# One 64-token chunk left out of the last levels of a blocked triangular inverse, in a two-block model on one Trainium2 core

## The chip, the cores and the metric

The kernel runs on one core of a Trainium2 chip, as a single program. A core has a matrix engine (TensorE, in the profile PE, its weight loads PEld), a vector engine (VectorE, DVE), a scalar engine (ScalarE, ACT), GpSimd (POOL), and SyncE (SP), which here only issues DMA transfers. Each engine works through its own instruction stream in order and waits on semaphores that the others raise. The metric is the device time of one execution in microseconds (us), as the median of several runs; lower is better.

## What is computed

Two model blocks run one behind the other on 512 tokens of width 1024. The first has an RWKV-7 mixer (32 heads of 64) and a latent attention mixer; the second a convolution and Fourier mixer and a grouped-query attention mixer. Only the RWKV-7 scan matters here. 16 learned tokens stand ahead of the 512 of the input, so it runs over 528 tokens:

```
h = jnp.concatenate([meta, x], axis=1)          # 16 + 512 tokens
...
def _wkv7_scan(r, decay, k, v, a_vec, b_vec):   # per head, S is 64 x 64
    def step(S, inp):
        r_t, w_t, k_t, v_t, a_t, b_t = inp
        sa = jnp.einsum('bhij,bhj->bhi', S, a_t)
        S = S * w_t[:, :, None, :] + sa[..., None] * b_t[:, :, None, :] + v_t[..., None] * k_t[:, :, None, :]
        return S, jnp.einsum('bhij,bhj->bhi', S, r_t)
```

Inside a chunk of 64 tokens this recurrence can be solved at once: with N the strictly lower triangular 64x64 matrix of products of a and b, the chunk needs the inverse of (I - N), and after that only the state S is handed from chunk to chunk.

## The kernel before

The program has a chain of stages. Stage A (a loop over 16 pairs of heads, L572) makes the projections of every pair and stores the forms of a pair (a, r, b, k, v, gate, bonus, per chunk) in HBM. **Stage B** (`pe_pass`, `act_pass`, `dve_pass`, `pool_pass`) is the recurrent stage. Stage C (from L1097 on) and those behind it are projections, attention and the second block, and this change doesn't touch them.

Stage B takes a pair of heads at a time: one head on partitions 0 to 63, the other on 64 to 127 (`by_head` issues each matrix product once for either head). 528 tokens are padded in front by PAD = 48 to LP = 576, which makes NC = 9 chunks of C = 64. So the first chunk has 48 empty tokens and 16 real ones. The chunks are handled in GROUPS = 3 groups g of GC = 3 chunks; `grp(g)` are a group's chunks and `flat(g)` its columns. `group(out, lhsT, rhs, chunks, done)` (L756 to L759) issues the products of all its chunks into one PSUM bank.

The stage is a sequence of passes, `passes(eng, body)`: pass i handles three pairs at once, the forms, inverse and a, k, b, v rows of pair i (`inv`), the walk over the nine chunks with the state of pair i - 1 (`scan`), and the normalisation of pair i - 2 (`post`). Passes 0 and 1 are written out, the passes 2 to 15 are the body of a loop of 7 turns with two passes each (L1037), passes 16 and 17 are written out again. `schedule` writes the order of the items of a pass by hand and `merged` spreads the 18 steps of the walk evenly among them; every engine goes through the same list and does what it has to do of each item.

The items that matter here, for pair i:
- `rows` n: product with the identity that turns a form into token rows; n = 0 to 2 are v, 3 to 5 k, 6 to 8 b, 9 to 11 a. ScalarE copies them out (L905), a into `a_tok` (in the profile a_rows).
- The inverse is built by doubling. `start` makes W (`xw[:, W_OF + par]`), GpSimd makes X and `n_lvl[:, lv]`, which are N masked to the blocks that join at level lv = 0 to 4 (blocks of 2, 4, 8, 16 and 32 tokens). Then at every level: `E` (lv, g) multiplies N of the level by W into `inv_bank[g]` and ScalarE copies it to `e_all` (L912); `XW` (lv, g) multiplies X by E (the corrections of X, into the bank's first half, not at the last level) and E by X (those of W, into the second half), and VectorE adds both halves to X and W in one instruction (L976), at the last level W alone (L979). In the profile X and W are the tile x_w and all PSUM banks are "wide".
- `A` g multiplies the a rows by W into a_hat (L915), which the walk of the next pass uses from chunk 1 on (L777: `if c > 0`).
- the walk of chunk c: products into u, y and state, ScalarE copies u (L889) and y (L892), VectorE updates the state (L943, L946, L949).

The matrices are 32-bit. In the profile a 64x64 product of one head stands as two weight loads (PEld) and two matmuls (PE), so that one product of a group of three chunks for both heads is a row of "x12". GpSimd (the masked N and X) and SyncE (the loads of forms) do in every pass what they did.

## Time and profile before

| | us |
|---|---|
| median of 3 runs | 2703.03 |
| lowest and highest of them | 2698.32 and 2703.87 |
| the profiled execution | 2701.88 |
| its span, first to last instruction | 2700.1 |

| stretch of the span | what runs | PE busy |
|---|---|---|
| 0 to 540 us | norm, stage A | 484.89 |
| 540 to 1345 us | stage B, the recurrent stage | 632.12 |
| 1345 to 2700 us | stage C and all behind it | 1160.08 |

The views used below are: a table of the engines' busy time in chosen stretches, with the granted TensorE clock; the chain of work that ended last, in order of time; the DMA queues of a stretch; the timeline, which merges equal instructions that follow each other (start, length in us, what, x count, and in brackets the engine's idle time ahead of it and what ended it); the waits, grouped; and groups of instructions with their mean duration. "issue" is time in which an engine waited for nothing that the profile shows. Instruction code that the engines fetch appears as a DMA queue of the kind "instruction".

### The profile page before, as it was taken

How to read it: one execution, taken by the hardware profiler on the slowest of the kernel's cores; microseconds unless marked ns; L12 is line 12 of the kernel's file. 1: busy time of each engine (PE TensorE's matmuls, PEld its weight loads, DVE VectorE, ACT ScalarE, POOL GpSimd, SP SyncE). 2: the span in 40 equal slices, each digit the busy share in tenths (PEclk: the TensorE clock that was granted, in tenths of full speed). 3: DMA queues.
4: the chain of work that ended last, by engine and by line, in shares of the span. 5: the costliest groups of instructions: out<-in, count | busy, mean ns of one | idle time of the engine just before them, and what ended most of it. 6: DMA issues, size and time to landing. Idle time of an engine off the chain costs nothing.

```text
span 2700.1 us, 67991 instructions
## 1 busy us (share of the span) xinstructions
PE 2277.1 (84%) x27094; PEld 1973.2 (73%) x27094; DVE 1338.5 (50%) x1907; ACT 786.2 (29%) x1899; POOL 1204.8 (45%) x708
## 2 busy tenths in 40 slices
PE   6799999987787887777686799999989499888776
PEld 5698898877777777777685796777779376565555
DVE  6666666634444444444444631445431544538655
ACT  1623323333333333333321222233311202111331
POOL 1465665531312213113385682222167588675234
PEclk8899999999999999999797899999989799999998
DMA  2234343431212112111221122000012221121001
GB/s 81 88 148 157 134 163 143 148 122 34 78 43 72 52 43 81 43 48 55 103 80 54 55 86 70 32 31 16 31 47 93 73 93 62 63 70 59 28 0 62
DMA packets 66824, 198.59 MB, mean 74 GB/s; under 512 B 26784, under 2 KB 29088, under 8 KB 62240
## 3 DMA queue, kind: packets, MB, share of 16 engines
q1 hardware_dynamic: 66592, 195.24, 20.8%
q8 instruction: 177, 2.90, 0.4%
q14 instruction: 55, 0.45, 0.1%
HBM read 156.24 MB, written 38.99 MB: 72 GB/s over the span
## 4 chain that ended last, share of the span: by engine, by line
PE 75%; DVE 10%; issue 8%; ACT 4%; POOL 1%; DVEq 0%; ACTq 0%; DMA 0%; SPq 0%; POOLq 0%
PE wide L754 22%; PE wide L1146 11%; PE wide L1147 11%; PE wide L1148 11%; PE wide L1622 4%; PE wide L355 4%; PE wide L1718 2%; PE wide L1682 2%; PE wide L1683 1%; PE wide L1507 1%; DVE mixed_in L325 1%; PE wide L1702 1%; PE wide L1970 1%; DVE normed L1284 1%; PE wide L2196 1%
## 5 line engine op out<-in xcount | busy, mean ns | idle before, releaser
L1013 POOL TENSOR_TENSOR n_levels<-n,masks 128x192 f32<-128x192 f32 (+1 forms) x96 | 115.5, 1219 | 576.0 <-ACT n L901 575.9
L1146 PE MATMUL wide<-mixed_high,w_high_rwkv_in 128*128 128x264 f32 x720 | 212.0, 294 | 29.1 <-ACT log_decay L435 20.2
L976 DVE TENSOR_TENSOR x_w<-wide,x_w 128x384 f32<-128x384 f32 x192 | 107.1, 558 | 207.7 <-PE wide L754 201.2
L1148 PE MATMUL wide<-mixed_high,w_low_rwkv_in 128*128 128x264 f32 x720 | 206.2, 286 | 0.0
L1147 PE MATMUL wide<-u_low_second,w_high 128*128 128x512 f32 x464 | 185.1, 399 | 0.0
L1170 POOL TENSOR_TENSOR w_high<-weights,con 128x1024 fp32r<-128x1024 f32 x60 | 147.5, 2459 | 74.6 <-PE wide L1148 64.7
L1263 DVE TENSOR_TENSOR sq_sum<-sq_sum,squares 128x528 f32<-128x528 f32 (+1 forms) x54 | 87.3, 1617 | 178.0 <-ACT squares L1228 178.0
L754 PE MATMUL wide<-e,x_w 64*64 64x64 f32 x2880 | 138.8, 219 | 43.5 <-issue 43.5
L355 PE MATMUL wide<-mixed_in,weights 128*128 128x264 f32 x672 | 158.9, 395 | 13.6 <-DVE mixed_in L325 12.0
L1146 PEld LDWEIGHTS wide<-mixed_high,w_high_rwkv_in 128*128 128x128 f32 x720 | 137.8, 191 | 37.4 <-ACT log_decay L435 26.5
L1173 POOL TENSOR_TENSOR w_low<-weights,w_high 128x1024 fp32r<-128x1024 f32 x60 | 157.7, 2628 | 4.7
L355 PEld LDWEIGHTS wide<-mixed_in,weights 128*128 128x128 f32 x672 | 128.9, 193 | 40.9 <-issue 9.5
L754 PEld LDWEIGHTS wide<-e,x_w 64*64 64x64 f32 x2880 | 113.6, 135 | 50.0 <-issue 50.0
L531 POOL TENSOR_TENSOR w_high_rwkv_in<-weights,con 128x1024 fp32r<-128x1024 f32 x45 | 107.7, 2394 | 72.0 <-PE wide L1148 71.3
L1148 PEld LDWEIGHTS wide<-mixed_high,w_low_rwkv_in 128*128 128x128 f32 x720 | 137.8, 191 | 0.0
L754 PE MATMUL wide<-x_w,n_levels 64*64 64x64 f32 x2880 | 132.5, 219 | 5.7 <-issue 5.3
L754 PE MATMUL wide<-eye,forms_in 64*64 64x64 f32 x2304 | 107.3, 220 | 21.5 <-issue 17.7
L754 PE MATMUL wide<-forms_in 64*64 64x128 f32 (+1 forms) x1728 | 113.9, 284 | 11.6 <-issue 8.8
L534 POOL TENSOR_TENSOR w_low_rwkv_in<-weights,w_high_rwkv_in 128x1024 fp32r<-128x1024 f32 x45 | 116.6, 2591 | 3.5
L1810 POOL COPY v_now<-v_rows 16x128 f32 (+1 forms) x16 | 4.5, 282 | 254.6 <-PE wide L1718 210.0
L1622 PE MATMUL wide<-latents,weights 128*128 128x264 f32 x512 | 116.6, 386 | 0.9 <-ACT v_rows L1542 0.9
L1146 PE MATMUL wide<-u_high_mla,w_high_mla 128*128 128x264 f32 x368 | 106.5, 289 | 12.7 <-DVE u_low_mla L1197 10.4
(321 smaller groups left out, 6813.3 us busy)
## 6 DMA issues: line engine op xcount, KB each, us to landing
weights<-in_stream SPq DMA_DIRECT2D x200, 512.0 KB, 3.3
forms<-form SPq DMA_DIRECT2D x16, 2020.5 KB, 6.3
forms_in<-forms SPq DMA_DIRECT2D x16, 1440.0 KB, 7.3
gate_bonus<-forms SPq DMA_DIRECT2D x16, 576.0 KB, 4.2
r_of_pair<-forms SPq DMA_DIRECT2D x16, 288.0 KB, 4.0
mixed<-gate_bonus SPq DMA_DIRECT2D x14, 264.0 KB, 2.1
gated<-mixed SPq DMA_DIRECT2D x14, 264.0 KB, 5.3
x<-in_tokens SPq DMA_DIRECT2D x4, 528.0 KB, 4.9
```

What stands on the lines that cost most here:

```text
L355: mm = pe.matmul(dst[:, b, 0:HALF], ring.slot(load)[:, k * P:(k + 1) * P], rhs[:, k, b * HALF:(b + 1) * HALF], start=k == 0, stop=k == kt - 1)
L531: pool.tensor_tensor(w_in[0][:, at, :].rearrange("p (k n) -> p k n", k=KD), ring.slot(load).rearrange("p (k n) -> p k n", k=KD), ones.unsq ...
L534: pool.tensor_tensor(w_in[1][:, at, :], ring.slot(load), w_in[0][:, at, :].bitcast(F32), ALU.subtract).then_inc(w_split, 1)
L754: mm = pe.matmul(out[rows], lhsT[rows], rhs[rows], start=start, stop=stop)
L976: dve.tensor_tensor(both, inv_bank[g][:, 0:2 * n].rearrange("p (s n) -> p s n", s=2), both, ALU.add).then_inc(q["xw_added"], 1)
L1013: return pool.tensor_tensor(n_lvl[:, first:last, grp(g), :], n_all[:, grp(g), :].unsqueeze(1).to_broadcast([P, n, GC, C]), b_con[:, 1 + fi ...
L1146: pe.matmul(dst, w[0], x[0], start=start, stop=False)
L1147: pe.matmul(dst, w[0], x[1], start=False, stop=False)
L1148: return pe.matmul(dst, w[1], x[0], start=False, stop=stop)
L1170: pool.tensor_tensor(w_hi[:, load % 2, :].rearrange("p (k n) -> p k n", k=KD), ring.slot(load).rearrange("p (k n) -> p k n", k=KD), ones.u ...
L1173: pool.tensor_tensor(w_lo[:, load % 2, :], ring.slot(load), w_hi[:, load % 2, :].bitcast(F32), ALU.subtract).then_inc(w_split, 1)
L1622: mm = pe.matmul(dst[:, b, 0:HALF], w[:, k * P:(k + 1) * P], latents[:, k0 + k, b * HALF:(b + 1) * HALF], start=k == 0, stop=k == kt - 1)
```

## The change

Nothing in the order of the items or in the loops is changed. The first chunk has 16 real tokens at its end, so blocks of 16 and of 32 tokens join nothing there but empty ones. `live(g, lv)` gives the chunks that take part: chunks 1 and 2 where g = 0 and lv is at least SHORT = 3, otherwise the whole group. With it, in every pass with `inv`:

- `rows` 9 (a rows of group 0) does two chunks in place of three, on TensorE and ScalarE, since the walk doesn't use a_hat of chunk 0;
- `E` (3, 0) and (4, 0) do two chunks, with their copies;
- `XW` (2, 0) does X of two chunks and W of three; (3, 0) both of two chunks; (4, 0) W of two chunks;
- `A` 0 does two chunks, with its copy;
- on VectorE the addition of (2, 0) becomes two instructions, X of 128 columns and W of 192, those of (3, 0) and (4, 0) get shorter.

```diff
--- before.py
+++ after.py
@@ -630,6 +630,23 @@
 
         def flat(g):
             return slice(g * GC * C, (g + 1) * GC * C)
+
+        REAL0 = C - PAD
+        SHORT = (REAL0 - 1).bit_length() - 1
+
+        def live(g, lv=LEVELS):
+
+            return slice(1, GC) if g == 0 and lv >= SHORT else grp(g)
+
+        def live_cols(chunks):
+            return slice(chunks.start * C, chunks.stop * C)
+
+        def width_of(chunks):
+            return (chunks.stop - chunks.start) * C
+
+        def some(ap, chunks):
+
+            return ap[:, 0:width_of(chunks)].rearrange("p (c n) -> p c n", n=C)
 
         def f_of(par_):
             ar = b_f[:, par_, 0:2 * LP].rearrange("p (c s n) -> p c s n", c=NC, s=2)
@@ -823,7 +840,7 @@
                     else:
                         pe.wait_ge(q["token_rows"], 12 * i + arg - 1)
                     begin()
-                    group(odd_bank[(arg + 1) % 2], lambda c: src[:, c, :], lambda c: eye[:], grp(arg % 3), token_mm)
+                    group(odd_bank[(arg + 1) % 2], lambda c: src[:, c, :], lambda c: eye[:], live(0) if arg == 9 else grp(arg % 3), token_mm)
                 elif item == "K":
                     if arg < 2:
                         pe.wait_ge(q["token_rows"], 12 * i + arg + 2)
@@ -848,7 +865,7 @@
                         if lv == 1:
                             pe.wait_ge(q["n_level"], 6 * i + GROUPS + g + 1)
                     begin()
-                    group(inv_bank[g], lambda c: n_lvl[:, lv, c, :], of(w), grp(g), e_mm)
+                    group(inv_bank[g], lambda c: n_lvl[:, lv, c, :], of(w), live(g, lv), e_mm)
                 elif item == "XW":
                     lv, g = arg
                     pe.wait_ge(q["e_rows"], 15 * i + 3 * lv + g + 1)
@@ -856,8 +873,8 @@
                         pe.wait_ge(q["x_start"], 6 * i + 2 * g + 2)
                     begin()
                     if lv < LEVELS - 1:
-                        group(inv_bank[g], lambda c: e_all[:, c, :], of(x), grp(g), None)
-                    group(inv_bank[g][:, GC * C:], of(x), lambda c: e_all[:, c, :], grp(g), xw_mm)
+                        group(inv_bank[g], lambda c: e_all[:, c, :], of(x), live(g, lv + 1), None)
+                    group(inv_bank[g][:, GC * C:], of(x), lambda c: e_all[:, c, :], live(g, lv), xw_mm)
                 elif item == "A":
                     if arg == 0:
                         pe.wait_ge(q["token_rows"], 12 * i + 12)
@@ -867,7 +884,7 @@
                         pe.wait_ge(q["a_rows"], GROUPS * i + 1)
                     pe.wait_ge(q["xw_added"], 15 * i + 12 + arg + 1)
                     begin()
-                    group(odd_bank[(arg + 1) % 2], lambda c: a_tok[:, c, :], of(w), grp(arg), a_mm)
+                    group(odd_bank[(arg + 1) % 2], lambda c: a_tok[:, c, :], of(w), live(arg), a_mm)
                 elif item == "post":
                     if arg == 0:
                         pe.wait_ge(Y_DVE.sem, Y_DVE.at(i - 2, 5))
@@ -902,17 +919,18 @@
                 elif item == "rows":
                     wait_heads(act, token_mm, 12 * i + arg + 1)
                     dst = (v_tok[:, par_], k_tok[:, par_], b_tok[:, par_], a_tok)[arg // 3]
-                    act.activation(dst[:, grp(arg % 3), :], three(odd_bank[(arg + 1) % 2]), ACT.Copy).then_inc(q["token_rows"], 1)
+                    chunks = live(0) if arg == 9 else grp(arg % 3)
+                    act.activation(dst[:, chunks, :], some(odd_bank[(arg + 1) % 2], chunks), ACT.Copy).then_inc(q["token_rows"], 1)
                 elif item == "M":
                     wait_heads(act, m_mm, GROUPS * i + arg + 1)
                     act.activation(mv[:, par_, grp(arg), :], three(odd_bank[(arg + 1) % 2]), ACT.Copy).then_inc(q["m_rows"], 1)
                 elif item == "E":
                     lv, g = arg
                     wait_heads(act, e_mm, 15 * i + 3 * lv + g + 1)
-                    act.activation(e_all[:, grp(g), :], three(inv_bank[g]), ACT.Copy).then_inc(q["e_rows"], 1)
+                    act.activation(e_all[:, live(g, lv), :], some(inv_bank[g], live(g, lv)), ACT.Copy).then_inc(q["e_rows"], 1)
                 elif item == "A":
                     wait_heads(act, a_mm, GROUPS * i + arg + 1)
-                    act.activation(a_hat[:, par_, grp(arg), :], three(odd_bank[(arg + 1) % 2]), ACT.Copy).then_inc(q["a_rows"], 1)
+                    act.activation(a_hat[:, par_, live(arg), :], some(odd_bank[(arg + 1) % 2], live(arg)), ACT.Copy).then_inc(q["a_rows"], 1)
                 elif item == "square":
                     act.wait_ge(Y_DVE.sem, Y_DVE.at(pp, 2))
                     act.activation(y_ln[:], y_ctr[:], ACT.Square).then_inc(Y_ACT.sem, 1)
@@ -972,11 +990,18 @@
                     if lv < LEVELS - 1:
                         if lv == 0:
                             dve.wait_ge(q["x_start"], 6 * i + 2 * g + 2)
-                        both = xw[:, par_::2, flat(g)]
-                        dve.tensor_tensor(both, inv_bank[g][:, 0:2 * n].rearrange("p (s n) -> p s n", s=2), both, ALU.add).then_inc(q["xw_added"], 1)
+                    chunks, m = live(g, lv), width_of(live(g, lv))
+                    if width_of(live(g, lv + 1)) == m and lv < LEVELS - 1:
+                        both = xw[:, par_::2, live_cols(chunks)]
+                        dve.tensor_tensor(both, inv_bank[g][:, 0:2 * n].rearrange("p (s n) -> p s n", s=2)[:, :, 0:m], both,
+                                          ALU.add).then_inc(q["xw_added"], 1)
                     else:
-                        one = xw[:, W_OF + par_, flat(g)]
-                        dve.tensor_tensor(one, inv_bank[g][:, n:2 * n], one, ALU.add).then_inc(q["xw_added"], 1)
+                        if lv < LEVELS - 1:
+                            kept = live(g, lv + 1)
+                            x = xw[:, X_OF + par_, live_cols(kept)]
+                            dve.tensor_tensor(x, inv_bank[g][:, 0:width_of(kept)], x, ALU.add)
+                        one = xw[:, W_OF + par_, live_cols(chunks)]
+                        dve.tensor_tensor(one, inv_bank[g][:, n:n + m], one, ALU.add).then_inc(q["xw_added"], 1)
                 elif item == "centre":
                     dve.wait_ge(q["y_rows"], 9 * pp + 9)
                     dve.tensor_reduce(y_sum[:], y_rows[:, par_], AX_X, ALU.add).then_inc(Y_DVE.sem, 1)
```

TensorE, in the first pass of the loop's body (the start of level 3), before. `x_w,n_levels` is an `E`, `x_w,e` with `e,x_w` an `XW`, `eye,forms_in` a `rows`; one row for one head and chunk stands here where the profile has two instructions:

```order
L754 MATMUL wide<-x_w,n_levels 64x64 [waits b_xw_added]
L754 MATMUL wide<-x_w,n_levels 64x64 x5
L824 REGISTER_ALU
L754 MATMUL wide<-eye,forms_in 64x64 [waits b_token_rows]
L754 MATMUL wide<-eye,forms_in 64x64 x5
L754 MATMUL wide<-x_w,n_levels 64x64 [waits b_xw_added]
L754 MATMUL wide<-x_w,n_levels 64x64 x5
L780 REGISTER_ALU
```

and now:

```order
L771 MATMUL wide<-x_w,n_levels 64x64 [waits b_xw_added]
L771 MATMUL wide<-x_w,n_levels 64x64 x3
L841 REGISTER_ALU
L771 MATMUL wide<-eye,forms_in 64x64 [waits b_token_rows]
L771 MATMUL wide<-eye,forms_in 64x64 x3
L771 MATMUL wide<-x_w,n_levels 64x64 [waits b_xw_added]
L771 MATMUL wide<-x_w,n_levels 64x64 x5
L797 REGISTER_ALU
```

The `E` and the `rows` of group 0 have two head products less each; rows, waits and order are the same.

VectorE, in the same pass, the additions of level 2 for groups 0 to 2 and the walk's step between them, before:

```order
L976 TENSOR_TENSOR x_w<-wide,x_w 128x2x192 [waits b_xw_mm1,b_xw_mm0]
L622 REGISTER_ALU
L976 TENSOR_TENSOR x_w<-wide,x_w 128x2x192 [waits b_xw_mm1,b_xw_mm0]
L622 REGISTER_ALU
L976 TENSOR_TENSOR x_w<-wide,x_w 128x2x192 [waits b_xw_mm1,b_xw_mm0]
L622 REGISTER_ALU
L945 REGISTER_ALU [waits b_s_mm1,b_s_mm0]
L946 SCALAR_TENSOR_TENSOR state<-wide,p_chunk,state_decayed 128x64 [waits b_s_decayed]
```

and now:

```order
L1002 TENSOR_TENSOR x_w<-wide,x_w 128x128 [waits b_xw_mm1,b_xw_mm0]
L1004 TENSOR_TENSOR x_w<-wide,x_w 128x192
L622 REGISTER_ALU
L996 TENSOR_TENSOR x_w<-wide,x_w 128x2x192 [waits b_xw_mm1,b_xw_mm0]
L622 REGISTER_ALU
L996 TENSOR_TENSOR x_w<-wide,x_w 128x2x192 [waits b_xw_mm1,b_xw_mm0]
L622 REGISTER_ALU
L963 REGISTER_ALU [waits b_s_mm1,b_s_mm0]
L964 SCALAR_TENSOR_TENSOR state<-wide,p_chunk,state_decayed 128x64 [waits b_s_decayed]
```

One instruction of VectorE is more, ahead of the addition of group 1.

## Rows read from the trace of the kernel before

**Rows 1.** Busy time (us, x count) by stretch: stage B, one turn of its loop.

```profile
core 0: us, PE busy (x) PEld busy (x) DVE busy (x) ACT busy (x) POOL busy (x), PEclk, DMA share, GB/s
540.00:1345.00 805.00, 632.12 (x17692) 601.23 (x17692) 356.73 (x765) 287.41 (x940) 188.00 (x205) 0.95 0.20 64
818.40:916.30 97.90, 78.09 (x2218) 74.59 (x2215) 44.69 (x97) 36.00 (x118) 21.31 (x24) 0.97 0.19 57
```

**Rows 2.** Chain that ended last, 917 to 963: start us, us, what.

```profile
917.22 3.40 issue
920.62 7.01 PE wide L754 x124
...
934.46 0.33 ACT m_v L908
...
938.51 3.77 PE wide L754 x121
942.28 0.82 issue
```

**Rows 3.** DMA queues by stretch: stage B; stage A's loop; 949.5:952.

```profile
q8 instruction: 150, 2.46, 1.3%
...
q1 hardware_dynamic: 12610, 58.11, 39.2%
...
q8 instruction: 1, 0.02, 2.9%
```

**Rows 4.** PEld, 887.0:914.2: busy and count; idle time; code fetched in it.

```profile
887.00:914.20 27.20, 22.10 (x728) 1.00 0.02 4
...
PEld wide L754 <- issue: 5.5, 7, 1.8
...
q8 instruction: 6, 0.10, 1.4%
```

**Rows 5.** Timeline of PEld: two products in full flow; branch; second stop behind it.

```profile
945.32 0.44 PEld L754 LDWEIGHTS wide<-x_w,e 64*64 64x64 f32 x12
945.66 0.44 PEld L754 LDWEIGHTS wide<-e,x_w 64*64 64x64 f32 x12
...
920.59 0.32 PEld L754 LDWEIGHTS wide<-m_v,x_w 64*64 64x64 f32 x4 [3.95 <-issue]
...
934.90 0.46 PEld L754 LDWEIGHTS wide<-v_rows_rwkv,k_with_a_r 64*64 64x64 f32 x12 [0.76 <-issue]
...
938.51 0.25 PEld L754 LDWEIGHTS wide<-x_w,e 64*64 64x64 f32 x5 [1.59 <-issue]
```

**Rows 6.** PEld behind the loop's branch: busy (x count), granted clock, DMA share, GB/s.

```profile
920.30:938.30 18.00, 14.76 (x343) 0.86 0.33 103
920.30:924.00 3.70, 3.41 (x46) 0.50 0.98 245
```

**Rows 7.** Waits of PE in 540:1345, and of PEld in the turn 818.4:916.3.

```profile
PE wide L754 <- issue: 138.5, 135, 4.0
PE wide L754 <- ACT a_hat L915: 9.1, 23, 0.7
...
PEld wide L754 <- issue: 23.0, 25, 4.1
```

**Rows 8.** Groups by form in 540:1345: busy us, mean ns, idle before.

```profile
L976 DVE TENSOR_TENSOR x_w<-wide,x_w 128x384 f32<-128x384 f32 x192 | 107.1, 558 | 207.7 <-PE wide L754 201.2
L979 DVE TENSOR_TENSOR x_w<-wide,x_w 128x192 f32<-128x192 f32 x48 | 15.9, 351 | 3.9 <-PE wide L754 3.4
L912 ACT ACTIVATE e<-wide 128x192 f32<-128x192 f32 x240 | 79.3, 331 | 108.0 <-PE wide L754 104.5
L889 ACT ACTIVATE u_rows<-wide 128x64 f32<-128x64 f32 x144 | 32.3, 224 | 125.2 <-PE wide L754 124.1
```

**Rows 9.** Chain that ended last, behind the stage, 1338 to 1358.

```profile
1349.00 1.39 DVE gate_bonus L999
...
1352.03 2.56 DVE z_low L1453 x2
```

## The prediction

> **What bounds the kernel now.** I read the busy time by stretch first [rows 1]. Stage B takes 805 of 2700 us, and TensorE is busy for 632 of them, VectorE for 357, ScalarE for 287. One turn of the loop, two passes, is 97.9 us with 2215 matmuls. Next the chain of work that ended last [rows 2]: in this stage it runs over TensorE nearly everywhere, and its matmuls come in portions of 120 or so, each portion 3.8 us long and followed by a stop in which it waits for nothing that the profile shows (0.82 us behind the portion at 938.51).
>
> The DMA queues tell what the stops are [rows 3]. In stage B, 150 pieces of instruction code are loaded, 2.46 MB, so 16.4 KB each; stage A's loop, whose body is short, has none in 400 us. 17692 matmuls to 150 loads is 118. In a stretch of full flow, 887.0 to 914.2 [rows 4], there are 728 matmuls and 6 code loads, 121.3 for each, and 5.5 us of idle time, 0.92 for each load. A load itself takes 2.9% of 16 engines over 2.5 us, 1.16 us [rows 3]; the request comes late enough in a portion that 3.8 us of work don't cover it. So a portion costs 27.20 / 6 = 4.53 us, of which 3.6 are issue time and 0.92 the stop. TensorE in this stage is bound by the number of its instructions, in two ways: by issuing them and by having them fetched.
>
> Waits on other engines are small: 9.1 us for a_hat's copy is the largest such row of the stage, against 138.5 us of unexplained stops [rows 7]. In one turn the stops and the branch make 23.0 us [rows 7].
>
> The Trainium skill (Runtime: NRT & Kernel Launch, Instruction fetch mechanics) says that code comes in blocks of 16 KiB, 256 instructions, which fits 121 matmuls with their weight loads and a dozen sequencer instructions. It also says that the fetch is mostly hidden; by that the stops shouldn't be there. The trace disagrees, with 0.92 us for each.
>
> **Issue time.** Over levels, rows and A the change drops one chunk at eight places of a pass: `rows` 9, `E` (3,0), `E` (4,0), X of `XW` (2,0), X and W of `XW` (3,0), W of `XW` (4,0), `A` 0. A group product of three chunks is x12 in the profile, so a chunk is 4 matmuls, and a pass loses 32 matmuls and 32 weight loads. One group product follows the other after 0.34 us [rows 5], 28 ns for a matmul; over the stretch of full flow it is 22.10 / 728 = 30.4 ns [rows 4]. I take 29.3: 32 x 0.0293 = 0.94 us a pass, and 16 passes have an inverse: **-15.0 us** (14.5 to 15.6). It is on the path because TensorE is the engine that ends last throughout; it would be hidden only where TensorE then waits for a copy.
>
> **Stops in the two written-out passes.** Passes 0 and 1 lose 64 matmuls together, 64 / 121 = 0.53 of a portion: 0.53 x 0.92 = **-0.5 us**.
>
> **Stops in the loop.** Here the place in the portion counts. Code is fetched anew in every turn: behind the branch TensorE stands for 3.95 us [rows 5]. From there to 938.30 there are 343 matmuls [rows 6], that is two whole portions and about 100 matmuls, so the loop begins some 21 matmuls into a portion. With 64 fewer ahead of it, it begins 64 earlier, with only about 40 of the first portion left. Its body is 64 shorter as well; together 128 matmuls and 128 weight loads, in full flow just over one portion. So the loop's end keeps its place in a portion, and a turn has as many stops as before, 2215 / 121 = 18. Their number doesn't change, only what stands around them:
> - First portion behind the branch. Its clock is granted at 0.50, the lower level (1.2 GHz), after the idle time of the branch, and the DMA engines are full with the forms (share 0.98) [rows 6]; 46 matmuls take 3.4 us. Today 100 slow matmuls cover the load of the next portion; 40 won't quite. Cost between 0 and the 1.59 us of the longest stop near there [rows 5]; I take +0.4, since 3.4 us is near the 3.6 us that leave 0.92, and the request after a branch comes at once. The second portion gets slower to cover too: +0.3 (0 to 0.9).
> - Third portion. Today it has TensorE's wait of 0.76 us for m_v in its first half, at 934.90, and then a stop of 1.59 [rows 2, 5]. The wait moves to the very end of a portion, 64 matmuls earlier, where it runs while code is on its way. Gain between 0 and 1.6; I take 1.3, wait and stop overlapping.
> - The end of the first pass has waits on a_hat copies and slow products too; there the boundaries shift by 32 matmuls. Between -1.5 and +0.5; I take -0.4, as waits now lie later in a portion.
> - The other 14 stops lie behind similar products before and after: 0, and 14 times ±0.05.
>
> Sum -1.0 us a turn. The distances of the five ends from the values taken, added as squares since they don't depend on each other, are 2.2 to the bad side (1.2, 0.6, 1.3, 0.9, 0.7) and 1.4 to the good one (0.4, 0.3, 0.3, 1.1, 0.7): +1.2 to -2.4 a turn. Times 7 turns **-7 us** (-17 to +8).
>
> **VectorE and ScalarE.** The addition of (2,0) was one instruction of 558 ns. Now it is one of 192 columns, 351 ns [rows 8], and one of 128, which by the difference of these two rows (207 ns for 192 columns) is about 282 ns, an estimate: 75 ns more, and some 50 ns of gap. That of (3,0) shrinks from 384 to 256 columns, about 420 ns, and that of (4,0) to 282. Copies of 128 columns lie between 331 and 224 ns [rows 8], about 278. Ahead of these additions VectorE idles for 201 us in all, waiting for TensorE; so the longer one is covered. But behind it stand the additions of groups 1 and 2 and the walk's state step, and `E` (3,1) now follows 0.12 us sooner. If the cover is gone, a pass pays the 0.13 us and the 0.12 us: 0 to 0.25, and below zero it can't go since no wait on x_w of note exists to be shortened [rows 7]. I take +0.03 a pass, **+0.5 us** (0 to 4).
>
> **What is behind the stage** moves as a whole: the last walk step is followed by the gate, its product and the low parts for stage C (1349.00, 1352.03) [rows 9], which start from what pass 17 makes. GpSimd, SyncE and the later loops have no instruction changed. The code of four written passes is 4 x 64 instructions shorter, so behind the stage portions begin where they did.
>
> **Sum:** -15.0 - 0.5 - 7 + 0.5 = -22 us. The profiled execution is 2701.88 us (span 2700.1), giving 2679.9; it lies 1.15 under the median of 2703.03, so the predicted median is **2681 us**. All terms at their good ends give -15.6 - 0.5 - 17 = -33, 2670, which I lower to 2668 for stops that are each a little shorter; at their bad ends with a moderate 1.5 on VectorE -14.5 - 0.5 + 8 + 1.5 = -5.5, 2697.
>
> **The rivals.**
> *Only the issue time.* The stops are as long as before in sum and the shift of the loop's start neither gives nor takes: -15 to -16, 2688 us. For it: the number of stops a turn stays 18. Against it: the third stop of a turn has an evident cause. By the skill's rule that fetching is hidden it would be just this time. Chance 0.24.
>
> *Slower: the new boundaries are worse.* Place: the 18 stops of a turn. Their length depends on where slow products and waits lie in a portion, and goes up to 1.8 us against a mean of 0.92 [rows 4]. The change saves 2 x 0.94 = 1.9 us of issue a turn; it is eaten when a stop is longer by 1.9 / 18 = 0.105 us on average, that is above 1.03. At 1.17 us each a turn costs 4.5 - 1.9 = 2.6 more, 18 us in all, 2720 us. For it: half of the first portion's cover is gone and clock and DMA are at their worst there. Against it: one or two stops can do that, not 18. Chance 0.05.
>
> *No change: TensorE waits in place of issuing.* `E`, its copy (331 ns), `XW`, its addition (558 ns) and the next `E` hang on each other [rows 8]. If at every level group 0 were late already, the 0.94 us a pass would turn into waits for x_w and e: about 2701 us. For it: VectorE and ScalarE wait for TensorE in short pieces all the time, so margins are small. Against it: copies and additions of group 0 get shorter too, and TensorE's largest wait of this kind is 9.1 of 805 us, with none for x_w or e among the large ones [rows 7]. Chance 0.07.
>
> *More than the good end*, below 2668, if most stops get shorter: 0.04.
>
> **How the numbers follow.** The forecast, 2668 to 2697 without the issue-only case, has 0.58; issue only 0.24; no change 0.07; slower 0.05; the big gain 0.04; a small gain above 2697 has 0.02. The range 2668 to 2697 holds the first two, 0.82. A measurement of this kernel tells about 0.2%, 5.4 us, from no change. Faster by more: 0.58 + 0.24 + 0.04 + 0.02 = 0.88; same 0.07; slower 0.05.
>
> **What would show it.** In the changed kernel's profile: 512 fewer matmuls and weight loads in stage B (17180); one code load fewer at most; a turn of 95 to 96.5 us in place of 98; portions of 120 matmuls as before; a short new stop about 3.5 us behind each branch, and no stop of 1.6 us behind the m_v wait. L1002 at some 282 ns, L1004 at 351 ns. It is wrong if TensorE shows waits for x_w or e of more than 5 us in sum, if the stops of a turn add up to over 22 us, or if a stage behind 1345 changes its length.

## The result and the profile after

The changed kernel takes 2715.8 us (median of 20 runs, 2705.33 to 2724.97). The kernel before, timed beside it on the same chip, takes 2704.37 us (20 runs, 2696.99 to 2716.75). The ratio is 1.0038, 95% interval [1.0027, 1.005], so the change costs some 10 us. The forecast of 2681 us, its range and its sign were wrong.

The profiled execution of the changed kernel took 2722.28 us, with a span of 2720.5, 20.4 more than that of before. Of these, 10.6 lie in stage B and are the subject of this text (counted from its first to its last matmul it takes 818.7 us, where before takes 808.1). 8.2 lie behind it, in 6252 matmuls that the change does not touch, at a granted clock of 0.92 against 0.94. In the twelve other kernels below, the part behind the stage takes 1351.9 to 1358.3 us with the same code, and 1360.3 here. I count this part as spread: the profiled execution lies 6.5 us above the kernel's own median, and the ratio of the medians leaves room for the stage's 10.6 and not for 20. It was not tested.

First come the busy times by stretch: stage B, then one turn of its loop, then the part behind the stage. The columns are as in [rows 1].

```profile
541.00:1360.00 819.00, 625.17 (x17212) 597.34 (x17214) 356.31 (x784) 284.65 (x941) 189.91 (x206) 0.93 0.20 64
822.20:922.20 100.00, 76.30 (x2153) 73.30 (x2152) 44.91 (x99) 35.76 (x118) 21.39 (x24) 0.95 0.18 56
...
1360.20:2720.50 1360.30, 1171.35 (x6252) 942.42 (x6248) 621.21 (x808) 319.00 (x689) 732.86 (x367) 0.92 0.16 55
```

The instructions went away as forecast: TensorE has about 512 matmuls fewer, and is busy for less. The stage is longer all the same. A turn has 64 matmuls fewer and takes 100 us where [rows 1] had 97.9. So it is idle time that grew. These are the waits of TensorE in the stage and of PEld in that turn:

```profile
PE wide L771 <- issue: 158.0, 118, 5.4
...
PEld wide L771 <- issue: 26.7, 24, 5.0
```

"Waited for nothing that the profile shows" rose from 138.5 to 158.0 us, and in the turn from 23.0 to 26.7 [rows 7]. No wait for x_w or e stands among the large ones. The DMA queues of the stage give five code loads more than the 150 of [rows 3]:

```profile
q8 instruction: 155, 2.54, 1.3%
```

Where the time is lost shows in the chain of work that ended last, 876 to 890:

```profile
875.92 1.69 PE wide L771 x37
877.62 0.11 issue
877.72 2.75 PE wide L771 x74
...
881.03 1.45 PE wide L771 x32
882.48 3.21 issue
885.69 4.35 PE wide L771 x65
```

A stop of 3.21 us has no counterpart before, where the longest inside a turn was 2.5. It stands behind the first pass of a turn. The PEld timeline, in the form of [rows 5], has it in six of the seven turns; the seventh is the last row here:

```profile
684.09 2.42 PEld L771 LDWEIGHTS wide<-forms_in 64*64 64x64 f32 x24 [4.44 <-issue]
...
783.81 2.42 PEld L771 LDWEIGHTS wide<-forms_in 64*64 64x64 f32 x24 [3.34 <-issue]
...
885.69 1.93 PEld L771 LDWEIGHTS wide<-forms_in 64*64 64x64 f32 x24 [3.35 <-issue]
...
985.04 2.28 PEld L771 LDWEIGHTS wide<-forms_in 64*64 64x64 f32 x24 [3.07 <-issue]
...
1087.22 2.06 PEld L771 LDWEIGHTS wide<-forms_in 64*64 64x64 f32 x24 [3.90 <-issue]
...
1192.56 1.62 PEld L771 LDWEIGHTS wide<-forms_in 64*64 64x64 f32 x24 [3.62 <-issue]
...
1288.42 1.28 PEld L771 LDWEIGHTS wide<-forms_in 64*64 64x64 f32 x24 [0.88 <-issue]
```

What the DMA engines do at that place is in the queues of 877.7 to 883.2, and then of 883.2 to 884.6, with the issue that falls into the first stretch between them (KB, us to landing):

```profile
q1 hardware_dynamic: 1520, 2.01, 106.5%
...
forms_in<-forms SPq DMA_DIRECT2D x1, 1440.0 KB, 6.9
...
q1 hardware_dynamic: 19, 0.07, 12.1%
q8 instruction: 1, 0.02, 4.4%
```

For 5.5 us the data queue holds the engines full, with 2.01 MB, most of it the 1440 KB of forms of the next pair; no code is loaded. Only when that load runs out (it lands at 884.83) does one piece of code come, from 883.38 on, and TensorE goes on at 885.69. In undisturbed portions of full flow the next piece of code starts to load 1.8 to 2.7 us after a portion began. Here it started 5.66 us after the beginning at 877.72.

The last turn is the one where no pair is left to be loaded, and so a control that the program brings along. SyncE's queue has the three small loads at this place and no forms_in (start, length, what); behind it stands the whole turn:

```profile
1280.13 0.33 SPq L694 DMA_DIRECT2D gate_bonus<-forms  x1
1280.57 1.44 SPq L686 DMA_DIRECT2D r_of_pair<-forms  x1
1282.05 1.60 SPq L687 DMA_DIRECT2D p_chunk<-forms  x1
```

```profile
1228.80:1324.60 95.80, 74.86 (x2159) 71.67 (x2155) 45.61 (x100) 35.75 (x118) 21.39 (x24) 0.96 0.15 43
```

The stop is 0.88 us, and the turn takes 95.8 us, where the same turn of before takes 98.5: in this one turn the forecast (95 to 96.5) came true. The five ahead of it take 100.0 to 104.3. One turn is a weak witness: with the load cut in all turns (below) they average 97.8.

The stop costs twice, because the clock falls behind it. First the portion ahead of the stop, then the stretch behind it:

```profile
877.70:882.40 4.70, 4.45 (x119) 4.29 (x119) 3.19 (x8) 2.10 (x7) 4.54 (x8) 1.00 1.10 365
885.70:889.00 3.30, 3.30 (x48) 3.30 (x50) 1.12 (x2) 0.21 (x2) 2.69 (x2) 0.58 0.03 5
```

The granted clock was 1.00 (2.4 GHz) and is 0.58, near the lower level (1.2 GHz), after 3.2 idle us: 69 ns for a matmul in place of 37.

The second place is the loop's branch. Timeline of PEld, and the code loaded in 922.2 to 926.9:

```profile
927.43 0.32 PEld L771 LDWEIGHTS wide<-m_v,x_w 64*64 64x64 f32 x4 [5.16 <-issue]
...
930.90 0.30 PEld L771 LDWEIGHTS wide<-forms_in 64*64 64x64 f32 x5 [0.22 <-issue]
...
936.48 0.13 PEld L771 LDWEIGHTS wide<-u_rows,b_rows 64*64 64x64 f32 x1 [0.79 <-issue]
```

```profile
q8 instruction: 2, 0.03, 4.9%
```

TensorE stands for 5.16 us behind the branch where it stood for 3.95 [rows 5]. Two pieces of code are in the air, where the same stretch of before has one. It is so at all six branches that are taken from 721 on: two loads start 0.65 to 1.26 us behind the branch. At the seventh, where the loop is left, a single load starts 0.74 us behind it. In the kernel before a single one starts 0.93 to 1.05 us behind each.

**How the place in a portion is counted.** In the trace's records of TensorE's sequencer (matmuls, weight loads and all others) the ends of portions lie exactly 256 instructions apart: a portion is one piece of code, below a block. Counting back from the first of them, the loop of before begins 31 instructions into a block of 256. With a body of 4710 instructions it ends 133 into one. The changed kernel begins 128 earlier, at 159 of the block before, and its body has 4582, so it ends at 133 as well. From the same records I split a turn into the branch, the stops at ends of blocks, all other gaps over 0.14 us, and the rest, which is issue. Means of six turns, in us (the last two columns: time at the lower clock, code loads a turn):

| kernel | turn | branch | stops | other gaps | issue | low clock | loads |
|---|---|---|---|---|---|---|---|
| before | 98.64 | 3.83 | 18.46 | 5.25 | 71.11 | 6.8 | 19 |
| changed | 100.58 | 4.96 | 20.94 | 4.83 | 69.85 | 10.2 | 20 |
| difference | +1.94 | +1.13 | +2.48 | -0.42 | -1.26 | +3.4 | +1 |

Six turns at +1.94 are +11.6 us. What lies ahead of them (passes 0 and 1 and the first turn) takes 179.6 us against 179.5, what lies behind them 35.6 against 36.7. That is the stage's +10.6.

### The profile page after: what moved, and what is told of

Read it like the earlier page. It is cut to its first block, busy times and chain, and to the rows that moved or that the text cites. A ratio compares the mean times of both kernels' runs of the same rounds, so it can differ in the third digit from the quotient of the medians.

```text
span 2720.5 us, 66983 instructions
## 1 busy us (share of the span) xinstructions
PE 2283.7 (84%) x26582; PEld 1982.7 (73%) x26582; DVE 1333.7 (49%) x1923; ACT 782.8 (29%) x1899; POOL 1205.0 (44%) x708
## 4 chain that ended last, share of the span: by engine, by line
PE 57%; issue 10%; DVE 6%; ACT 2%; POOL 2%; POOLq 1%; DVEq 0%; ACTq 0%
PE wide L771 19%; PE wide L1171 8%; PE wide L1172 8%; PE wide L1173 8%; PE wide L1647 4%; PE wide L1743 2%; PE wide L1707 2%; PE wide L1708 1%; PE wide L1532 1%; PE wide L1727 1%; PE wide L1995 1%; DVE normed L1309 1%; PE wide L2221 1%; DVE inv_rms L1296 1%; ACT odd_probs L2238 1%
## 5 line engine op out<-in xcount | busy, mean ns | idle before, releaser
L996 DVE TENSOR_TENSOR x_w<-wide,x_w 128x384 f32<-128x384 f32 (+1 forms) x176 | 95.9, 545 | 175.4 <-PE wide L771 170.1
L771 PEld LDWEIGHTS wide<-forms_in 64*64 64x64 f32 x1728 | 99.7, 155 | 31.9 <-issue 31.3
L771 PE MATMUL wide<-x_w,e 64*64 64x64 f32 x2176 | 108.9, 220 | 15.7 <-issue 15.7
L771 PEld LDWEIGHTS wide<-eye,forms_in 64*64 64x64 f32 x2240 | 91.1, 137 | 42.3 <-issue 42.3
L771 PEld LDWEIGHTS wide<-x_w,n_levels 64*64 64x64 f32 x2752 | 114.5, 139 | 4.8 <-issue 4.8
```

What stands on the lines that cost most here:

```text
L771: mm = pe.matmul(out[rows], lhsT[rows], rhs[rows], start=start, stop=stop)
L996: dve.tensor_tensor(both, inv_bank[g][:, 0:2 * n].rearrange("p (s n) -> p s n", s=2)[:, :, 0:m], both, ALU.add).then_inc(q["xw_added"], 1)
```

## The experiments

Three theories stood at the start. **Collision**: a code load is asked for just as the 1440 KB load of forms_in runs, and comes late. **Wasted request**: a loop that ends 133 instructions into a block has the next block, behind the loop, on its way when the branch comes, and the loop's first block queues behind it. **The work itself**: VectorE's longer chain or the shorter copies make TensorE late in a way that the trace hides.

### Moving the code without changing the work

Fillers ahead of the loops shift TensorE's code. They are 115 to 243 increments of a semaphore that nobody waits for. Each costs 0.153 us, and in all padded kernels stage B begins 8 to 12 us later. So the stage, not the total, is to be compared.

```diff
         def pe_setup(pe):
+            for _ in range(128):
+                pe.sem_inc(q["turn"], 1)
             pe.wait_ge(con_loaded, 32)
```

The changed kernel with 128 fillers, so that its loop begins where that of before does, at 31, and ends at 5:

> The changed kernel with 128 one-step filler instructions at the very start of TensorE's stream, where it waits 10 us for data anyway. They move all code of TensorE behind them by half a block of 256, so that the loop of the recurrent stage begins 31 instructions into a block, as in the kernel before. Theory (the place of the code decides): the stop of 3.2 us behind the end of the first pass and the 2.6 us ones go, a turn of the loop takes 95.5 to 97.5 us in place of 100.2 to 104.3, in all 2682 to 2694 us, below both kernels. Rival (what is left of the work, or VectorE's extra instruction, costs the time): the place is nothing, 2712 to 2720 us.

The kernel before with the same fillers. It begins at 159 and ends at 5:

> The kernel before, all its work kept, with the same 128 fillers. The loop then begins 159 instructions into a block, as in the changed kernel, and its body of 4710 reaches over 19 block ends in place of 18. Theory (place): a turn gets 2 to 5 us longer, 2715 to 2735 us, with a stop of about 3 us near the loads of forms in the first pass, though no work was changed. Rival (the work or VectorE's split makes the changed kernel slow): 2700 to 2708 us as before.

The changed kernel with 115, which begins at 18 and ends at 248, so that a turn crosses 17 ends of blocks:

> The changed kernel with 115 fillers: the loop begins 18 instructions into a block, and its body of 4582 ends at 248 of a block, so a turn crosses 17 block ends in place of 18. Theory (place and number of blocks): one stop less a turn than with 128 fillers, turns of 94.5 to 97 us, 2676 to 2692 us. If a block requested ahead past the loop's end costs 1 us at the branch, it appears here too, with 19 code loads a turn. Rival (work): 2712 to 2720 us.

The changed kernel with 123 fillers there and 120 more behind `pe_setup(pe)`. It begins at 146 and ends at 120, just under half a block:

> The changed kernel with 243 fillers (123 at the start, 120 ahead of the first weight product, where TensorE waits 8.4 us): one block less 13, so that all code lies nearly as in the changed kernel, but the branch at the loop's end stands 120 instructions into its block instead of 133. Theory (the code load requested just ahead of the branch delays the load of the branch's target): 19 code loads a turn in place of 20, TensorE stands 3.9 us at the branch in place of 4.9, turns 1 us shorter, 2706 to 2712 us; the stop of 3.2 us behind the first pass stays. Rival (the longer stand at the branch is from the target's place in its block): 20 loads and 4.9 us as before, 2716 us.

All four ran on one chip with the kernel before, which took 2711.63 us there (25 runs):

| kernel | begins, ends | median | ratio, 95% | stage B | turn | branch | stops | issue | loads |
|---|---|---|---|---|---|---|---|---|---|
| changed + 128 | 31, 5 | 2702.45 | 0.997 [0.9952, 0.9989] | 796.1 | 97.02 | 3.79 | 16.95 | 69.42 | 19 |
| before + 128 | 159, 5 | 2717.33 | 1.0018 [1.0005, 1.0031] | 807.2 | 98.73 | 3.71 | 17.90 | 70.92 | 20 |
| changed + 115 | 18, 248 | 2698.18 | 0.9941 [0.9924, 0.9959] | 794.2 | 96.54 | 3.45 | 16.84 | 69.67 | 19 |
| changed + 243 | 146, 120 | 2720.11 | 1.0029 [1.0013, 1.0045] | 814.1 | 99.38 | 3.78 | 20.47 | 70.44 | 19 |

Three of the four totals lie 6 to 9 us above the range expected of them: changed + 128, changed + 115 and changed + 243. The fillers make the stage begin later, and before itself is 7 us slower in this set; the turns, branches and loads of these three came near what was expected. Before + 128 fell into its expected range (2715 to 2735) by luck: the theory had its turns 2 to 5 us longer, and they are not (98.73 against 98.64).

Stage B takes 808.1 us before and 818.7 changed. With the same work at another place it takes 794.2. So 24 us hang on where the loop lies in the blocks, more than on the work left out. The last kernel separates the two causes. Its branch is back at the old length with one code load less a turn, and the long stop is still there. These are the waits of its stage, the timeline's rows of a long stop and of the branch that follows, and the code loads of 926.6 to 931, behind that branch:

```profile
PE wide L773 <- issue: 159.6, 121, 4.0
```

```profile
890.22 1.67 PEld L773 LDWEIGHTS wide<-forms_in 64*64 64x64 f32 x16 [3.60 <-issue]
...
930.95 0.32 PEld L773 LDWEIGHTS wide<-m_v,x_w 64*64 64x64 f32 x4 [4.12 <-issue]
```

```profile
q8 instruction: 1, 0.02, 1.4%
```

So the branch's 1.1 us and the long stop are separate things. And the number of code loads is a poor measure: this kernel has 149 in the stage and takes 814.1 us, before + 128 has 156 and takes 807.2.

The kernel before bears the same start, 159, without harm to the stage (807.2 against 808.1). Its body is 128 instructions longer, so the ends of its blocks near the first pass's end fall elsewhere. A begin at 159 is not bad as such. What counts is where an end of a block meets the load.

### Taking the load away

The other way round: code and place stay, and the forms of pairs 3 to 15 are loaded with their v columns alone, 288 KB in place of 1440. The a, r, b and k columns in the buffers are those of earlier pairs, so this leaves out four fifths of the load and computes something else from them at the same cost for the engines.

```diff
-            sp.dma_start(b_f[:, par_, :], forms[i, :, 0:5 * LP]).then_inc(forms_loaded[par_], 16)
+            n = F_V if not isinstance(i, int) or i > 2 else 0
+            sp.dma_start(b_f[:, par_, n:5 * LP], forms[i, :, n:5 * LP]).then_inc(forms_loaded[par_], 16)
```

In the changed kernel:

> The changed kernel with only a fifth of the forms (the v columns, 288 KB instead of 1440 KB) loaded for the pairs from 3 on; the others stay as an earlier pair left them, so the output differs. Place in the code blocks as in the changed kernel. Theory (the stop of 3.2 us in the tenth and eleventh block of a turn is a code load that queues behind the 1440 KB load): that stop falls to about 1.2 us, 2 us a turn less, stage B about 804 instead of 819, total about 2702 in place of 2716; the branch, with its two code loads, stays at about 5 us or loses at most 1. Rival (the long stop comes from the position of slow products alone): it stays at about 3.2 us and the total within 3 us of 2716.

In the kernel before:

> The kernel before with the same small load (the v columns alone for the pairs from 3 on; output differs). Control for the run above. Theory: here no code load queues behind the large load for long (largest stop of a turn 1.7 us), so it gains clearly less: 0 to 6 us, total 2698 to 2704, stage B 802 to 808. Rival (any code load beside bulk data is slower, whatever its place): as much as in the changed kernel, about 14 us.

Measured: changed 2695.66 us (2691.16 to 2701.73), ratio 0.9956 [0.9941, 0.9971]. Before 2706.81 (2699.02 to 2714.61), ratio 0.9999 [0.9983, 1.0016]. The same cut is worth nothing in the kernel before. The changed kernel goes from 1.0038 to 0.9956, that is 0.8%, 22 us; since the two ratios come from two sets of runs, the stage is the better witness: 798.1 against 818.7. It is more than the 14 us expected, since the clock comes back too. The same place of the trace, in the timeline of PEld and the stretches, of the changed kernel with the small load:

```profile
875.58 1.28 PEld L772 LDWEIGHTS wide<-forms_in 64*64 64x64 f32 x24 [0.60 <-issue]
```

```profile
875.60:878.60 3.00, 2.88 (x71) 2.77 (x73) 2.96 (x5) 0.80 (x2) 3.00 (x3) 1.00 0.02 5
```

The same 24 weight loads for forms_in begin after 0.60 us instead of 3.35 and at a clock of 1.00 instead of 0.58. On average of six turns this stop is 1.0 us, from 3.2 (the last turn, without the load, counted in). The branch stays at 4.89, as it should if it is another cause.

These two kernels also give the worth of the change once the collision is out of the way. Turn by turn the issue time is 69.22 against 71.10, both with 6.8 us at the lower clock: 1.88 us less. Median against median it is 11 us.

### The same bytes in five pieces

```diff
-            sp.dma_start(b_f[:, par_, :], forms[i, :, 0:5 * LP]).then_inc(forms_loaded[par_], 16)
+            for k in range(5):
+                cols = slice(k * LP, (k + 1) * LP)
+                sp.dma_start(b_f[:, par_, cols], forms[i, :, cols]).then_inc(forms_loaded[par_], 16)
...
-                        pe.wait_ge(forms_loaded[par_], turn_of(i, par_, 16))
+                        pe.wait_ge(forms_loaded[par_], turn_of(i, par_, 80))
```

In the changed kernel:

> The changed kernel with the 1440 KB load of the forms issued as five loads of 288 KB in a row, computing the same. Theory one (a code load waits for the end of the transfer that is in the queues ahead of it): it can now slip in between two pieces, the stop of 3.2 us falls to 1.2 to 2 us, total 2702 to 2710. Theory two (it waits for all that was issued before it, or for bandwidth): the stop stays at 3 us or more, total 2713 to 2720.

In the kernel before:

> The kernel before with the forms loaded as five transfers of 288 KB. Control for the split in the changed kernel, which gave 15 us. Theory: as with the small load, no gain here beyond 3 us, ratio 0.999 to 1.001. Rival: 10 us or more, so that the split is good in itself and says nothing of the change.

Measured: changed 2700.57 us (2692.79 to 2704.8), ratio 0.997 [0.9958, 0.9982], stage B 805.0. Before 2707.16, ratio 0.9993 [0.9983, 1.0003]. The total came out near what the first theory said (2702 to 2710), the ratio down by 0.7% in the changed kernel, and before gained nothing. But the stop did not go all the way: 2.4 us on average of six turns, from 3.2. That is 5 of the 11.6 us by which these six turns got shorter. The rest is spread over other stops and a little over 1 us a turn less at the lower clock, and was not explained, so part of the good total is luck. One of its longer ones:

```profile
978.92 1.28 PEld L773 LDWEIGHTS wide<-forms_in 64*64 64x64 f32 x24 [2.80 <-issue]
```

So neither theory of that expectation fits alone. A code load does get in ahead of the later pieces: in one turn it starts at 875.52 and takes 1.95 us, and of the five pieces, issued from 872.46 on, the first lands at 875.75 and the last at 880.45. But it starts only when gate_bonus (landed at 874.17), r_of_pair (873.92) and nearly all of the first piece are through. How exactly a code load takes its turn among the data packets is left open. The runs show only that it is late behind one large load, less so behind a small piece, and not at all when there is little data.

### A version without fillers

If the place decides, the cheapest filler is the work itself: passes 0 and 1, which are written out ahead of the loop, do their first chunk again, save for `rows` 9 and `A` 0 of pass 1. That puts 112 instructions back, and the loop begins at 15 and ends at 245 of a block.

```diff
-        def live(g, lv=LEVELS):
+        def live_in(i):
 
-            return slice(1, GC) if g == 0 and lv >= SHORT else grp(g)
+            def live(g, lv=LEVELS):
+                all_of = isinstance(i, int) and (i == 0 or i == 1 and lv < LEVELS)
+                return slice(1, GC) if g == 0 and lv >= SHORT and not all_of else grp(g)
+            return live
...
+            live = live_in(i)
```

The last line stands in the passes of TensorE, ScalarE and VectorE.

> The changed kernel, but the written-out passes 0 and 1 do their first chunk again (all but `rows` 9 and `A` 0 of pass 1), which puts 112 TensorE instructions back ahead of the loop. No filler. The loop then begins 15 instructions into a block of 256 instead of 159, and ends near the end of a block, so one stop a turn fewer, one code load a turn fewer, and the two long stops (second block of the first pass's end, branch with two loads in the air) should be gone. Theory (place of the loop in the blocks decides): a turn of about 96.5 us instead of 100.6, stage B about 795 instead of 819 even though some 1.7 us of work came back, total about 2690, ratio to before 0.995 (0.9935 to 0.9965). Rival (the change itself makes the loop slower, the fillers of the earlier runs helped in another way): about 2715 to 2718.

Measured: 2696.88 us (2689.97 to 2704.61), ratio 0.9952 [0.9938, 0.9967]; before took 2709.52 beside it. The ratio is the expected 0.995; the absolute time is 7 us above, 5 of which before shows as well in this set. It does more work than the changed kernel, and by the two ratios is 0.86% faster. It beats both kernels. Turn 97.46, branch 3.70, stops 17.28, other gaps 6.78, issue 69.69, no stop over 2.1 us. Its stage, with waits and code loads:

```profile
540.00:1342.00 802.00, 621.74 (x17272) 591.44 (x17272) 356.67 (x780) 286.87 (x941) 193.31 (x209) 0.94 0.20 65
```

```profile
PE wide L775 <- issue: 147.0, 130, 3.9
```

```profile
q8 instruction: 150, 2.46, 1.3%
```

The turn was expected at 96.5 and took 97.46: the other gaps are 1.5 us longer than before, as they are in three of the padded kernels (6.2 to 6.9; 4.7 in changed + 243). One of them is 1.2 us a pass ahead of `A` 0. In the trace the last addition of VectorE that `A` 0 needs starts at 864.85, behind 1.4 us of work on gate_bonus, and `A` 0 at 865.21, after 1.06 us of idle time. In before the same addition starts late too (868.07), but TensorE stands there in a stop for code until 868.53. A stop that vanishes uncovers the wait that ran beside it.

Both remedies together, and the pieces spread over the pass:

> Both remedies: the written-out passes 0 and 1 with their first chunk (the loop begins 15 instructions into a block) and the forms loaded as five transfers of 288 KB. Theory (the collision costs only where a code load is asked for just behind the large load, which is so in the changed kernel and not here, where no stop of a turn is above 1.6 us): little is left to gain, 0 to 4 us less than the 2697 us of the first remedy alone, ratio to before 0.9935 to 0.9955. Rival (smaller transfers help any code load): 15 us less, as in the changed kernel.

> As the run above, but in the loop the last four of the five transfers wait for the copies of E of levels 0 to 3 (`e_rows` 1, 4, 7 and 10 of the pass), so that they are spread over most of a pass in place of 7 us. Theory: a code load never has more than one such transfer ahead of it; no stop above 1.7 us; 0 to 5 us less than with the transfers in a row, as long as the forms land before the next pass, which they should by over 10 us. Rival (more code loads meet a transfer now, each a little later): same or up to 5 us more.

The first took 2699.58 us (2695.3 to 2705.68), ratio 0.9972 [0.9957, 0.9987]; the second, with `sp.wait_ge(q["e_rows"], 15 * (i - 1) + 3 * k - 2)` ahead of pieces 1 to 4, took 2709.89, ratio 1.0007 [0.9992, 1.0021]. The split in a row adds nothing: its ratio is no lower than that of the version without it (0.9952), and the 15 us of the rival (small transfers help any code load) are far outside its interval. The spread pieces cost 9 to 10 us, which neither side expected in that size. In the trace the stop of the second full block of a turn is 2.3 instead of 1.7 us, that of the eleventh 1.9 instead of 1.5, and stage B takes 808.4 instead of 798.0. Presumably the pieces now meet code loads at more places. That these meetings are the cause, and all of the 10 us, was not tested.

### VectorE's side alone

The kernel before with the addition of level 2, group 0 in two instructions, everything on TensorE where it was:

```diff
+                        if (lv, g) == (2, 0):
+                            x, one = xw[:, X_OF + par_, flat(g)], xw[:, W_OF + par_, flat(g)]
+                            dve.tensor_tensor(x, inv_bank[g][:, 0:n], x, ALU.add)
+                            dve.tensor_tensor(one, inv_bank[g][:, n:2 * n], one, ALU.add).then_inc(q["xw_added"], 1)
+                            continue
```

> The kernel before, but VectorE adds the corrections of X and of W of level 2, group 0 in two instructions of 192 columns in place of one of 384. TensorE has every instruction where it was. It holds what VectorE's side of the change can cost, rather more of it: two instructions of 351 ns for one of 558. Theory: +0.15 us a pass where nothing covers it, 0 to 3 us in all, ratio 0.999 to 1.0015. Rival (VectorE's longer chain is what made the changed kernel slower): 10 us or more.

Measured: 2708.1 us, ratio 1.0003 [0.9986, 1.0019], stage B 808.4 against 808.1. VectorE's part does not explain a loss of 10 us: the interval ends at 5. Nor do its other changes or the shorter copies: all of them are in changed + 128, changed + 115 and the version without fillers, which are faster than before. The groups by form show the two instructions, and no idle time ahead of the second:

```profile
L977 DVE TENSOR_TENSOR x_w<-wide,x_w 128x192 f32<-128x192 f32 x16 | 5.7, 358 | 17.9 <-PE wide L754 17.9
L978 DVE TENSOR_TENSOR x_w<-wide,x_w 128x192 f32<-128x192 f32 x16 | 5.6, 348 | 0.0
```

## Why the prediction was wrong, step by step

**Issue time, -15.0: right at an equal clock, not reached in the changed kernel.** 32 instruction pairs a pass were put at 0.94 us, so 1.88 a turn. With the collision away the two kernels differ by 1.88 (that it is the same to the last digit is chance). In the changed kernel itself it is 1.26, since the clock stands at its lower level for 10.2 us a turn in place of 6.8. That is 0.6 a turn, 4 us, which the sum didn't have.

**Stops in the written-out passes, -0.5.** Not resolved: the first turn, with its own stop of 4.44 us, can't be told from them in the 179.6 us above.

**Stops in the loop, -1.0 a turn: this is the step that failed.** The stops came out at +2.48, the branch at +1.13 and the other gaps, in which the m_v wait of the term stood, at -0.42. That is +3.2, off by 4.2 us a turn, 29 us in seven turns. By its parts:
- *First and second portion*, +0.4 and +0.3. The first stop is 0.8, from none (0.2 to 1.0, and once 2.6), the second 0.5 from 0.4. The forecast short new stop about 3.5 us behind the branch is there, at 930.90. Mechanism and size right.
- *Third portion*, -1.3. The stop went from 1.6 to 1.3 on average, and the m_v wait of 0.73 to 0.84 that stood ahead of it in every turn of before no longer stands by itself: in the changed kernel it falls 5 instructions ahead of the block's end and runs beside the stop. Together about -1.1. Mechanism and size right.
- *End of the first pass*, -0.4 within -1.5 to +0.5. Here stands the stop of 3.2 us, +1.8 against before and so far outside the term's range. The text took note of full DMA engines behind the branch [rows 6], and counted 343 matmuls from there, but never looked at the forms load in the other pass of the turn. Before, that place is half clear of it: the code load starts at 874.08, when the forms load has just been issued (873.64), and the portion ahead is full of slow products; the next code load starts at 879.70, as the forms land (880.24). TensorE stands there for 0.80 us in the turn shown below, 1.4 on average of six turns, 2.5 at most. After the shift a portion begins at 877.72 and the load is issued at 877.93. The row of before:

```profile
876.58 0.46 PEld L754 LDWEIGHTS wide<-forms_in 64*64 64x64 f32 x12 [0.80 <-issue]
```

- *The other 14 stops*, 0. They sum to much the same, within 0.3 us a turn.
- *The branch.* It had no term at all. The statement that the loop's end keeps its place in a block, 133, was right and taken as harmless. The number of stops a turn did stay 18, but the loads rose from 19 to 20 and the branch from 3.83 to 4.96. In full flow the next block starts to load 1.8 to 2.7 us into the 3.6 us in which a block is issued, so by these numbers it is asked for about half-way (an estimate), and 133 lies just there. The earlier of the two loads, at 0.65 to 0.77 us in most turns, fits the block behind the loop, since where the loop is left it comes alone; the later one, at 1.0, fits the loop's first block. Among the versions of the changed kernel it goes with the end: all three that end at 133 have the long branch (4.96, 4.89, 5.08), and those that end at 5, 120, 245 or 248 don't (3.45 to 3.79); nor does before + 128, which begins at 159 and ends at 5. But before ends at 133 by the same count, as do its versions with the small load, the split load and two additions, and all four have one load in the air and the short branch. So the end alone does not decide. Why the request comes just ahead of the branch in the one body and just behind it in the other, at the same place, is left open.

**VectorE, +0.5.** Right as far as can be told: 0.8 us (-3.8 to +5.1) in the run made for it. Durations by form in the changed kernel, stage B, were 292 ns for the 128 columns that had been put at 282, and 425 for 256 columns put at 420:

```profile
L996 DVE TENSOR_TENSOR x_w<-wide,x_w 128x256 f32<-128x256 f32 x16 | 6.8, 425 | 19.2 <-PE wide L771 19.2
...
L1002 DVE TENSOR_TENSOR x_w<-wide,x_w 128x128 f32<-128x128 f32 x16 | 4.7, 292 | 3.6 <-PE wide L771 3.0
L1004 DVE TENSOR_TENSOR x_w<-wide,x_w 128x128 f32<-128x128 f32 x16 | 4.6, 284 | 2.7 <-PE wide L771 2.7
```

**Behind the stage.** No instruction changed there. The prediction named a changed length there as a sign that it is wrong, and the profiled execution shows 8.2 us more, 2.0 above the longest of the twelve others. I take it for spread, as said above; no run tests it.

**The rivals.** The slower one named the right place, the 18 stops of a turn, and about the right price for a turn, 2.6 us against 1.94 measured. It got 0.05 because "one or two stops can do that, not 18" was taken as speaking against it. But one or two stops suffice when one of them meets a transfer of 7 us: the mean stop of a turn is 20.94 / 18 = 1.16 us. That this is so close to its 1.17 is luck: it started from 0.92, while the stops of a turn of before average 18.46 / 18 = 1.03, and it had no term for the branch. The five ends of the range were added as squares, as if no place could be worse than the worst stop seen before. The fault lies there: the bound for a stop was taken from those seen in one stretch at the old places, up to 1.8 us (other turns of before have one of 2.5), while a shift by half a block tries places that the trace of before doesn't show.

**The loading of code.** The trace shows one code load more a turn and a longer branch. The Trainium skill (Runtime: NRT & Kernel Launch, Instruction fetch mechanics) says that prefetch is purely sequential and that a taken branch outside the window stalls until the target is fetched; the two loads behind the branch at 922.2 and the 5.16 us for which TensorE stands agree with that. The same section of the Trainium skill says that crossing a block costs one tail bump, mostly hidden. By that the stops of a turn would be near zero; 18.46 us of 98.64 before, and 20.94 after, say otherwise.

## What to carry to other kernels

Where an engine's code does not stay loaded in a loop and its stops for code are a fifth of the time, taking instructions out moves every later end of a block: write down where in the blocks the loop begins and ends, and at which moments of a turn large data transfers run, and price the case that an end of a block meets one. Then treat the place as something to choose. Here putting 112 instructions of useless work back ahead of the loop turned a loss of 0.4% into a gain of 0.5%, and issuing one load of 1440 KB as five recovered four fifths of that without moving any code, though only a part of that gain is explained. A bound taken from the stops seen so far holds only while the places stay.

## What the runs showed of the hardware

- A code load asked for during a 1440 KB data load started 5.66 us after its block began, in place of 1.8 to 2.7, and the stops at that place were 3.1 to 3.9 us in five turns and 4.4 in the first. With the same bytes in five pieces the stop was 2.4 on average, with a fifth of the bytes 1.0.
- The granted clock, 1.00 in the portion ahead, was 0.58 behind a stop of 3.2 us. It stayed at 1.00 behind one of 0.60 at the same place.
- The same work took 794.2, 796.1, 814.1 or 818.7 us in this stage, by where its loop of 4582 instructions lay in blocks of 256.
- A loop's branch cost TensorE 3.45 to 3.87 us, on average of a kernel's turns, with one code load in the air and 4.9 to 5.1 with two.
